# Three 256-column matmuls into one 256-column sum, in the feature tiles of a two-layer hybrid encoder

## The reference

```python
h = rms_norm(x, ffn1_norm_pre[l])
h = swiglu(h, ffn1_w_gate[l], ffn1_w_up[l], ffn1_w_down[l])   # (silu(h @ w_gate) * (h @ w_up)) @ w_down
x = x + 0.5 * rms_norm(h, ffn1_norm_post[l])

h = rms_norm(x, mix_norm_pre[l])
proj = h @ w_in[l]                       # 1024 -> 2560, split into eight parts
y = concat([rglru(...), sliding_window_attention(...), differential_attention(...)]) @ w_out[l]
x = x + rms_norm(y, mix_norm_post[l])
# then the second feed-forward block, as the first
```

## Time and profile before

| | |
|---|---|
| median of three runs | 1111.56 us |
| profiled execution, span (all that is recorded of its own time) | 1110.8 us |
| PE busy | 1007.4 us, 91% |
| PE weight loads busy | 868.6 us, 78% |
| DVE busy | 703.0 us, 63% |
| ACT busy | 511.7 us, 46% |
| POOL busy | 91.0 us, 8% |
| mean granted clock of TensorE | 0.954 of full speed |
| DMA | 180.56 MB, 163 GB/s in the mean |

### The profile page before, as it was taken

The page is one execution under the profiler, slowest core; times in us unless marked ns, Lnnn a source line. Parts: engine busy times, 40 slices in busy tenths (PEclk is TensorE's granted clock), DMA queues, the critical chain, the costliest instruction groups (busy, mean ns, idle before and its releaser), DMA issues. The chain is left out here.

```text
span 1110.8 us, 15638 instructions
## 1 busy us (share of the span) xinstructions
PE 1007.4 (91%) x5486; PEld 868.6 (78%) x5486; DVE 703.0 (63%) x895; ACT 511.7 (46%) x646; POOL 91.0 (8%) x49
## 2 busy tenths in 40 slices
PE   7666999969998699999969999998799959999996
PEld 5555888858897688888858888887689848888885
DVE  4615556575778766556667566557667786556555
ACT  3414444434565454444445444444455534444442
POOL 1000000030302200000010000002040040000000
PEclk9887999989999799999979999999899969999999
DMA  5767555633335255555615655665243335565550
GB/s 168 224 90 261 189 189 189 227 114 114 134 117 169 76 189 188 186 192 182 203 54 192 216 178 183 195 218 180 75 134 134 127 102 154 187 191 186 189 170 39
DMA packets 137486, 180.56 MB, mean 163 GB/s; under 512 B 10488, under 2 KB 121208, under 8 KB 137440
## 3 DMA queue, kind: packets, MB, share of 16 engines
q1 hardware_dynamic: 136400, 177.31, 48.9%
q0 software_dynamic: 1040, 2.68, 1.7%
HBM read 177.35 MB, written 2.62 MB: 162 GB/s over the span
## 5 line engine op out<-in xcount | busy, mean ns | idle before, releaser
L447 PE MATMUL UP<-xT,whi 128*128 128x512 f32 x1648 | 588.6, 401 | 32.3 <-DVE wlo L986 18.1
L986 DVE TENSOR_TENSOR wlo<-raw,whi 128x2048 fp32r<-128x2048 f32 (+1 forms) x156 | 355.5, 2280 | 218.8 <-ACT whi L728 218.5
L449 PE MATMUL UP<-xT,wlo 128*128 128x256 f32 x1648 | 464.1, 282 | 0.0
L447 PEld LDWEIGHTS UP<-xT,whi 128*128 128x128 f32 x1648 | 312.1, 189 | 110.4 <-DVE wlo L986 27.3
L728 ACT ACTIVATE whi<-raw 128x2048 fp32r<-128x2048 f32 x162 | 306.0, 1890 | 167.5 <-PE Y L470 122.1
L449 PEld LDWEIGHTS UP<-xT,wlo 128*128 128x128 f32 x1648 | 313.6, 190 | 1.4
L470 PE MATMUL Y<-whi,hidT 128*128 128x512 f32 x640 | 178.8, 391 | 0.0
L470 PEld LDWEIGHTS Y<-whi,hidT 128*128 128x128 f32 x640 | 117.4, 188 | 24.6
L495 PE MATMUL UP<-ident 128*128 128x128 f32 x276 | 51.2, 360 | 53.6 <-DVE x L1059 28.8
L470 PE MATMUL Y<-wlo,hidT 128*128 128x512 f32 x320 | 99.4, 392 | 0.0
L495 PEld LDWEIGHTS UP<-ident 128*128 128x128 f32 x276 | 48.0, 267 | 57.9 <-DVE x L1059 30.3
(11 more groups left out here) (169 smaller groups left out, 804.1 us busy)
## 6 DMA issues: line engine op xcount, KB each, us to landing
raw<-in_ffn_w_gate SPq DMA_DIRECT2D x44, 1024.0 KB, 5.3
raw<-in_ffn_w_up SPq DMA_DIRECT2D x44, 1024.0 KB, 5.4
raw<-in_ffn_w_down SPq DMA_DIRECT2D x44, 1024.0 KB, 4.9
raw<-in_w_in SPq DMA_DIRECT2D x20, 1024.0 KB, 5.1
raw<-in_w_out SPq DMA_DIRECT2D x6, 1024.0 KB, 4.8
gains<-in_ffn_norm_pre SPq DMA_DIRECT2D x4, 512.0 KB, 4.8
gains<-in_ffn_norm_post SPq DMA_DIRECT2D x4, 512.0 KB, 5.5
raw<-in_w_out SPq DMA_DIRECT2D x4, 512.0 KB, 3.6
```

What stands on the lines that cost most here:

```text
L447: nc.tensor.matmul(dst[:, 0:2 * S], h[:, kt, c:c + P], xT[:, kt, :, :].rearrange("p h s -> p (h s)"), start=kt == 0, stop=False, skip_grou ...
L449: mm = nc.tensor.matmul(dst[:, S:2 * S], o[:, kt, c:c + P], xT[:, kt, 0, :], start=False, stop=kt == KT - 1, skip_group_check=True)
L986: V.tensor_tensor(wlo[:, slot, 0:n], raw[:, slot, 0:n], whi[:, slot, 0:n].bitcast(F32), ALU.subtract).then_inc(lo_ready, 1)
```

## The change

All three products of a feature tile now add up in the same 256 columns, by three matmuls of 256 columns per step. The copies of the small parts on ScalarE and the sums on VectorE go; tanh reads PSUM, and so do VectorE's two products. In the mixer VectorE copies the finished tile, without ScalarE. TensorE's gate banks are now free after `swished`, the up banks after `hid_ready`.

```diff
@@ feature_tile
-                    nc.tensor.matmul(dst[:, 0:2 * S], h[:, kt, c:c + P], xT[:, kt, :, :].rearrange("p h s -> p (h s)"),
+                    nc.tensor.matmul(dst[:, 0:S], o[:, kt, c:c + P], xT[:, kt, 0, :],
                                      start=kt == 0, stop=False, skip_group_check=True)
-                    mm = nc.tensor.matmul(dst[:, S:2 * S], o[:, kt, c:c + P], xT[:, kt, 0, :],
-                                          start=False, stop=kt == KT - 1, skip_group_check=True)
+                    for part in range(2):
+                        mm = nc.tensor.matmul(dst[:, 0:S], h[:, kt, c:c + P], xT[:, kt, part, :],
+                                              start=False, stop=part == 1 and kt == KT - 1, skip_group_check=True)
@@ TensorE, gate_up
-                        pe.wait_ge(gate_sum, pair0 + i)
+                        pe.wait_ge(swished, pair0 + i)
...
-                        pe.wait_ge(up_sum, pair0 + i)
+                        pe.wait_ge(hid_ready, pair0 + i)
@@ ScalarE, gate_parts (up_parts is gone)
-                        act.wait_ge(gate_sum, pair0 + i)
-                    nc.scalar.activation(gate_small[:, :, :], UP[:, 0:1024].rearrange("p (f c) -> p f c", f=2)[:, :, S:2 * S],
-                                         ACT.Copy).then_inc(gate_low, 1)
+                        act.wait_ge(swished, pair0 + i)
+                    nc.scalar.activation(tanh[:, :, :], UP[:, 0:1024].rearrange("p (f c) -> p f c", f=2)[:, :, 0:S],
+                                         ACT.Tanh, scale=0.5).then_inc(gate_tanh, 1)
                     lead()
...
-                    nc.scalar.activation(tanh[:, :, :], gate[:, :, :], ACT.Tanh, scale=0.5).then_inc(gate_tanh, 1)
@@ VectorE, gate_parts and up_parts
-                    V.tensor_tensor(gate[:, :, :], UP[:, 0:1024].rearrange("p (f c) -> p f c", f=2)[:, :, 0:S], gate_small[:, :, :], ALU.add).then_inc(gate_sum, 1)
                     lead()
 
                     dve.wait_ge(gate_tanh, pair0 + i + 1)
-                    V.scalar_tensor_tensor(gate[:, :, :], tanh[:, :, :], 1.0, gate[:, :, :], ALU.add, ALU.mult).then_inc(swished, 1)
+                    V.scalar_tensor_tensor(gate[:, :, :], tanh[:, :, :], 1.0, UP[:, 0:1024].rearrange("p (f c) -> p f c", f=2)[:, :, 0:S], ALU.add, ALU.mult).then_inc(swished, 1)
...
-                    dve.wait_ge(up_sum, pair0 + i + 1)
-                    V.scalar_tensor_tensor(hid[:, :, :], gate[:, :, :], 0.5, up[:, :, :], ALU.mult, ALU.mult).then_inc(hid_ready, 1)
+                    dve.wait_ge(unit_used, l * UNITS + k + 1 + RING)
+                    V.scalar_tensor_tensor(hid[:, :, :], gate[:, :, :], 0.5, UP[:, 1024:2048].rearrange("p (f c) -> p f c", f=2)[:, :, 0:S], ALU.mult, ALU.mult).then_inc(hid_ready, 1)
@@ VectorE, tile (ScalarE's copy of it is gone)
-                dve.wait_ge(tile_low, l * N_APART + FEATURE_TILE[q] + 1)
+                if t:
+                    dve.wait_ge(unit_used, l * UNITS + MIX0 + u + 1 + RING)
+                else:
+                    dve.wait_ge(first_tile, l * IN_UNITS + u + 1)
...
-                    ins = V.tensor_tensor(dst, bank(UP, t, 0, S), small, ALU.add)
+                    ins = V.tensor_copy(dst, bank(UP, t, 0, S))
```

More of the change, by code:

```diff
@@ L121, in program @@
         gate_small = sb("gate_small", [P, 2, S])
-        up_small = sb("up_small", [P, 2, S])
         gate = sb("gate", [P, 2, S])
@@ L126, in program @@
         hid = sb("hid", [P, 2, S])
-        tile_small = sb("tile_small", [P, 2, S])
         lx = sb("lx", [P, 2, 3 + S])
@@ L182, in program @@
         y_scaled = sem("y_scaled")
-        gate_low, up_low = sem("gate_low"), sem("up_low")
-        gate_sum, up_sum = sem("gate_sum"), sem("up_sum")
         gate_tanh, swished = sem("gate_tanh"), sem("swished")
         hid_ready, hid_hi, hid_lo = sem("hid_ready"), sem("hid_hi"), sem("hid_lo")
-        first_tile, tile_low, tile_sum, tile_copied = (sem(n) for n in ("first_tile", "tile_low", "tile_sum", "tile_copied"))
+        first_tile, tile_sum, tile_copied = (sem(n) for n in ("first_tile", "tile_sum", "tile_copied"))
         scores_done, logits_ready = sem("scores_done"), sem("logits_ready")
@@ L781, in gate_parts @@
                     if again:
-                        act.wait_ge(gate_sum, pair0 + i)
-                    nc.scalar.activation(gate_small[:, :, :], UP[:, 0:1024].rearrange("p (f c) -> p f c", f=2)[:, :, S:2 * S],
-                                         ACT.Copy).then_inc(gate_low, 1)
+                        act.wait_ge(swished, pair0 + i)
+                    nc.scalar.activation(tanh[:, :, :], UP[:, 0:1024].rearrange("p (f c) -> p f c", f=2)[:, :, 0:S],
+                                         ACT.Tanh, scale=0.5).then_inc(gate_tanh, 1)
                     lead()
-                    act.wait_ge(gate_sum, pair0 + i + 1)
-                    if again:
-                        act.wait_ge(swished, pair0 + i)
-                    nc.scalar.activation(tanh[:, :, :], gate[:, :, :], ACT.Tanh, scale=0.5).then_inc(gate_tanh, 1)
[L794 to L801, removed]
                 split(l, base + 2)
                 gate_parts(0, base, False, lambda: split(l, base + 3))
-                up_parts(0, base + 1, False)
                 if j == 0:
@@ L814, in pair @@
                     gate_parts(i, a, True, lambda: split_hi(l, a + 3, 2, count=i + third))
-                    up_parts(i, a + 1, True)
                     if spread:
@@ L839, in tile @@
                     return
-                if FEATURE_TILE[q] > 1:
-                    act.wait_ge(tile_sum, l * N_APART + FEATURE_TILE[q] - 1)
-                nc.scalar.activation(tile_small[:, FEATURE_TILE[q] % 2, :], bank(UP, t, S, 2 * S), ACT.Copy).then_inc(tile_low, 1)
             def exps(l, j, between=lambda: None):
@@ L1073, in gate_parts, with up_parts @@
                 def gate_parts(i, lead, again=True):
-                    dve.wait_ge(gate_low, pair0 + i + 1)
                     if again:
                         dve.wait_ge(hid_ready, pair0 + i)
-                    V.tensor_tensor(gate[:, :, :], UP[:, 0:1024].rearrange("p (f c) -> p f c", f=2)[:, :, 0:S],
-                                    gate_small[:, :, :], ALU.add).then_inc(gate_sum, 1)
                     lead()
                     dve.wait_ge(gate_tanh, pair0 + i + 1)
-                    V.scalar_tensor_tensor(gate[:, :, :], tanh[:, :, :], 1.0, gate[:, :, :], ALU.add, ALU.mult).then_inc(swished, 1)
[L1086 to L1090, removed]
+                    V.scalar_tensor_tensor(gate[:, :, :], tanh[:, :, :], 1.0, UP[:, 0:1024].rearrange("p (f c) -> p f c", f=2)[:, :, 0:S],
+                                           ALU.add, ALU.mult).then_inc(swished, 1)
+                def up_parts(i, k, lead):
                     lead()
                     dve.wait_ge(swished, pair0 + i + 1)
-                    dve.wait_ge(up_sum, pair0 + i + 1)
-                    V.scalar_tensor_tensor(hid[:, :, :], gate[:, :, :], 0.5, up[:, :, :], ALU.mult, ALU.mult).then_inc(hid_ready, 1)
+                    dve.wait_ge(unit_used, l * UNITS + k + 1 + RING)
+                    V.scalar_tensor_tensor(hid[:, :, :], gate[:, :, :], 0.5, UP[:, 1024:2048].rearrange("p (f c) -> p f c", f=2)[:, :, 0:S],
+                                           ALU.mult, ALU.mult).then_inc(hid_ready, 1)
                 if j == 0:
@@ L1103, in ffn @@
                 gate_parts(0, lambda: split(l, base + 3), again=False)
-                up_parts(0, lambda: small_parameters(l) if j == 0 else None)
+                up_parts(0, base + 1, lambda: small_parameters(l) if j == 0 else None)
                 def pair(i, last=False):
@@ L1110, in pair @@
                     gate_parts(i, lambda: split_lo(l, a + 3, 2))
-                    up_parts(i, lambda: None if last else split_lo(l, a + 4, 0))
+                    up_parts(i, a + 1, lambda: None if last else split_lo(l, a + 4, 0))
                 with dve.Fori(1, PAIRS - 1) as i:
@@ L1130, in tile @@
                         src, to = slice(HD * h, HD * h + HD), slice(HD * g, HD * g + HD)
-                        ins = V.tensor_tensor(swk[to, h, :], bank(UP, t, 0, S)[src], small[src], ALU.add)
+                        ins = V.tensor_copy(swk[to, h, :], bank(UP, t, 0, S)[src])
                 else:
```

1 line of the change is left out of this document (removed).

## The result

The changed kernel takes **1121.66 us**, the median of four runs (1119.55 to 1122.31), against 1111.87 for the kernel before beside it (four runs, 1110.14 to 1112.47). The ratio is 1.0088, with a 95% interval of 1.0073 to 1.0102: slower by 0.9%. The forecast was 1120.9. Beside those experiments one of 17 runs of the kernel before took 1996.75 us; no ratio uses it.

A forecast was written before the change was run, and what follows sets the result against it. TensorE's pace through its matmuls was taken as the bound. Terms of +9.1, +1.4 and -1.2 gave +9.3 us, 1120.1 on the profiled span and 1120.9 us for the median; range 1113.5 to 1127, ends 1116.6 and 1129.

The forecast's parts named there:

- The pace: TensorE's feature-tile steps: three 256-column matmuls take 0.3586 us, 0.0055 more than now, over 1648 steps +9.1 us (+6.9 to +11.9).
- The start of layer 0's first feed-forward: Pair 1 waits for the swished gate and starts 2.8 us later; between 0 and 2.8 arrives, taken as +1.4 us.
- The mixer: TensorE's 0.76 us wait for GpSimd's convolution ahead of the gates shrinks to about 0.2: -0.6 us per layer, -1.2 in all.
- The second feed-forward's start: Pair 1 just avoids waiting for the swished gate, 0.2 us to spare, table load out of the path: cost 0.
- Rival C: Starts of stages wait as well, the table load lying in the path: +2.2 us, 1123.1 us; chance 0.09.
- Rival A: Feature-tile steps: the third matmul, with the second's stationary operand, costs only its columns: -10.2 us, 1101.5 in all; chance 0.08.
- Rival B: Feature-tile steps keep 0.353 us, as dropping the 512/256 alternation pays for the third matmul: 1111.8 us; chance 0.12.

The follow-up runs named there:

- e1: The kernel before with the change's three 256-column matmuls alone, copies and sums kept with the copies delivering zeros: 1121.87 us, ratio 1.0090.
- e2: The kernel before with the change's evacuation and waits alone, old matmul widths, small products left out of the output: 1112.31 us, ratio 1.0012.
- e3: The kernel before with the 512-column matmul split into two of 256 into the bank's two halves, evacuation as before: 1121.93 us, ratio 1.0091.
- e4: The kernel before with each feature tile's eight 512-column matmuls first, then its eight 256-column ones: 1107.57 us, ratio 0.9956.
- e5: The kernel before with matmuls of one width in longer rows across a unit's two tiles, fewer changes of width: 1103.14 us, ratio 0.9935.
- e6: The kernel before with the 256-column matmul adding to the lower half of the tile, not the upper: 1112.66 us, ratio 1.0011.
- e7: The changed kernel once more, unaltered, on the same chip as e5 and e6: 1121.72 us, ratio 1.0099 to the kernel before.

## Why the prediction was right

It was right in sign, in size and in mechanism; that the sum came within 1 us is partly luck, since the small errors of its terms lie within the noise and cancel in part. By its own steps:

**The pace.** It was put at +9.1 us, and this term was too small. A 256-column matmul in feature tiles costs 0.1200, the upper end of the token tiles' 0.1191 to 0.1200, so a step takes 0.360 and not 0.3586. Taking the mean of the two token tiles was the slip: the second one starts quick, with nine matmuls in 1.06 us (0.118 each), and its last 13 take 1.56, 0.1200 each, like the first tile. The 0.3531 of before was that of the steady pair; over the whole trace a step of before took 0.3519 in the mean, since some took 0.347. Against that, a down tile behind 256-column matmuls takes 5.47 and not 5.50. In a steady pair the two errors cancel, so that the forecast of 16.98 us between down tiles came out to the digit, by luck. In the stages the term is +2.5 and +2.1 for the two second feed-forwards and about +2.3 for layer 1's first. In layer 0's first, only what lies behind the second wait for weights counts, since TensorE waits there until about 92 in either case. From there to the last matmul of the stage before takes 141.65 us and after 142.42, of which 4.5 and 2.9 are at 1.2 GHz; less half of these, it is 139.4 and 141.0, so +1.6. With +0.8 in each mixer (e1 against before) the term is about **+10**, inside the ends of +6.9 and +11.9. e1, which has this term alone, measured +10.6.

**The start of layer 0's first feed-forward.** It was put at +1.4, between 0 and 2.8. The forecast said that pair 1 would start 2.8 us later, and the changed kernel's rows seem to deny it, with 39.33 where it was 38.96:

```profile
31.44 1.91 ACT L725 ACTIVATE whi<-raw 128x2048 fp32r<-128x2048 f32 x1 [10.66 <-DMA raw<-in_ffn_w_gate]
...
38.42 0.68 DVE L1057 SCALAR_TENSOR_TENSOR gate<-tanh,UP 128x512 f32<-128x512 f32 x1
39.33 0.58 PE L443 MATMUL UP<-xT,wlo 128*128 128x256 f32 x1 [8.57 <-DVE gate L1057]
```

The weights landed earlier in this execution: their split began at 31.44, and at 33.91 in the profile of before. Counted from there pair 1 starts after 7.89 us in the changed kernel and 7.85 in e2, and after 5.05 before and 5.06 in e1: 2.8 later, as forecast. How much of it arrives is less sure. TensorE's next wait, for weights, ended at 89.98 to 92.00 in the profiles of the six kernels without the late start (before, e1, e3, e4, e5, e6), 91.08 in the mean, and at 92.01, 91.85 and 93.54 in the three with it (after, e7, e2), 92.47 in the mean: 1.4 later, where single executions lie up to 2 us apart. The medians agree as far as they go. e2 is 1.0 slower than before and has won 0.9 in the mixers, which leaves +1.9; the changed kernel is 0.2 faster than e1 and has won 0.9 there, which leaves +0.7; each has the noise of two medians on it. The +1.4 fits all of this, and the runs do not settle it closer.

**The mixer.** It was put at -0.6 per layer, and measured -0.5: 100.52 against 101.00 in e1, which has the same matmuls and the old evacuation. The wait ahead of the gates was forecast at about 0.2:

```profile
285.92 2.97 POOL L407 TENSOR_TENSOR xs<-xs,par 128x512 f32<-128x512 f32 x1
288.95 2.00 PE L642 MATMUL UP<-xs,lruw 128*128 128x256 f32 x8 [0.21 <-POOL xs L407]
```

It was 0.76 before and is 0.69 in e1, so the slower steps alone take 0.07 off it. In e2, with the old steps, it is 0.53 and 0.37 in the two layers. So it is the lighter evacuation that shortened it. This term and the one before roughly cancel, which is why e1 and the whole change come to the same.

**The second feed-forward's start.** It was put at 0, with 0.2 us to spare. The timelines of ScalarE, VectorE and TensorE in layer 0, as the earlier trace rows:

```profile
380.07 1.92 ACT L725 ACTIVATE whi<-raw 128x2048 fp32r<-128x2048 f32 x1
382.01 1.28 ACT L781 ACT_TABLE_LOAD   x1
386.13 0.60 ACT L781 ACTIVATE tanh<-UP 128x512 f32<-128x512 f32 x1 [2.83 <-PE UP L446]
...
390.77 0.68 DVE L1057 SCALAR_TENSOR_TENSOR gate<-tanh,UP 128x512 f32<-128x512 f32 x1
...
391.69 0.28 PE L443 MATMUL UP<-xT,wlo 128*128 128x256 f32 x1
```

The table load ran at 382.01, while ScalarE had nothing else to do, and not between the end of the tile and tanh. The swished gate ended at 391.45 and pair 1 started at 391.69, at the usual 0.12 behind the matmul ahead of it. **Rival C** falls with that. But the margin of 0.2 us that the prediction counted is used up. From the end of the gate to the start of pair 1 are 0.24 us, and in layer 0's first stage, where TensorE did wait for the same gate, it was 39.33 - (38.42 + 0.68) = 0.23. The other two places have 0.24 as well, with at most 0.1 us lost behind it. In e2, with the shorter steps of before, up to 0.3 us are lost at such a place. So the 0 came out, narrowly, and a split that lasts a little longer would make it a wait.

**Rival A**, the free second use of a stationary operand, falls by the changed kernel's own 0.24 us for two such matmuls and by e3. **Rival B** was half true. The usual step of before has 6 to 7 ns on top of the 0.3467 that its two matmuls take in rows (0.2267 + 0.120), and with equal widths they go. But the third matmul costs 13 ns on top of its columns, which is more than that gives back: 0.3467 + 0.0133 is the 0.360 that was measured. The Trainium skill's rule (TensorE: Matmul & The Clock Gate, section Back-to-back issue gap), which the page gives for a single matmul by itself, would have 0.109 us for 256 columns and 0.216 for 512. The runs show 0.120 and 0.2267, and these measurements decide.

## What to carry to other kernels

Where TensorE is the bound, count its instructions before anything else: here every fp32r matmul cost some 13 ns on top of its columns, and 114 us of work taken off the two other engines bought about 1 us in the mixers, which a later start of one pair took back. Price a new instruction by a row of the same kernel that already has its form, and measure a late start from the event that it depends on, not from the start of the span. If widths must be mixed, put matmuls of one width in rows and let neighbouring tiles meet at the same width; that was worth 8.4 us (e5) without a change to any other engine.

## What the runs showed of the hardware

- **A change of width costs.** Between rows of 256 and of 512 columns, the first five starts of the 512-column ones are late by 27 ns in all (e4, e5). In alternation a step of 512 and 256 mostly has 6 to 7 ns on top (0.353 us), but about one step in five of the kernel before has nothing (0.347), in stretches of up to 62 steps. I had put the step's 0.353 down to its two matmuls alone.
- **The cost on top of the columns is there at 2.4 GHz and not at 1.2 GHz.** Behind the wait in layer 0 TensorE has the lower clock, and a step takes 0.64 us, which is 768 columns at 1.2 GHz and nothing more, in the changed kernel as in the one before. So the changed kernel loses nothing in such stretches. The timeline of the changed kernel, before and after the clock rises:

```profile
40.13 0.41 PE L443 MATMUL UP<-xT,wlo 128*128 128x256 f32 x1
...
40.77 0.41 PE L443 MATMUL UP<-xT,wlo 128*128 128x256 f32 x1
...
44.57 0.28 PE L443 MATMUL UP<-xT,wlo 128*128 128x256 f32 x1
...
44.93 0.28 PE L443 MATMUL UP<-xT,wlo 128*128 128x256 f32 x1
```

- **Behind a short wait the lower clock came in some executions and not in others.** In e3 and e5 the wait ahead of the gates in layer 0's mixer was 0.68 and 0.77 us, and the eight matmuls behind it took nearly twice their time; in e4, with 0.76, they did not, but they did in its layer 1, with 0.77. In all, 3 of the 12 mixers with a wait of 0.68 to 0.77 us (before, e1, e3 to e6) have it. That the wait brings it was not tested. First a stretch of e3 around it (its granted clock is the 0.72, third from the end), then the gates of e3, e4 and e5 in TensorE's timeline:

```profile
286.00:292.00 6.00, 5.32 (x25) 4.48 (x25) 5.38 (x15) 0.91 (x3) 1.83 (x1) 0.72 0.63 212
```
```profile
287.89 3.55 PE L647 MATMUL UP<-xs,lruw 128*128 128x256 f32 x8 [0.68 <-POOL xs L411]
```
```profile
286.85 1.99 PE L646 MATMUL UP<-xs,lruw 128*128 128x256 f32 x8 [0.76 <-POOL xs L411]
```
```profile
284.95 3.52 PE L663 MATMUL UP<-xs,lruw 128*128 128x256 f32 x8 [0.77 <-POOL xs L411]
```

Such a mixer took 1.7 us longer (e3: 102.66 against 101.00 in e1). With the lighter evacuation the wait was 0.21, and the lower clock did not come in either profile of the changed kernel; six mixers (after, e7, e2) are too few to say that it can't. Grouped matmuls with the lighter evacuation of the mixer alone might therefore gain a little more; this was not tried.
